# Weight halves ahead of the inner norms, and orders elsewhere, in a two-layer decoder trunk

## The reference

```
for i in range(2):
    y = conv_deltanet_mixer(x, ...) if i == 0 else nsa_mixer(x, positions, ...)
    x = layer_norm(alpha * x + y, ln_mix_g[i], ln_mix_b[i])
    x = layer_norm(alpha * x + (silu(x @ gate) * (x @ up)) @ w_out, ln_ffn_g[i], ln_ffn_b[i])   # 5632 hidden
```

## Time and profile before

| | |
|---|---|
| three runs | 2394.88, 2398.44, 2401.35 us; median 2398.44 |
| profiled execution | 2397.81 us |
| its span, first to last instruction | 2396.0 us |
| PE busy | 2350.1 us (98%) |
| DVE, ACT, POOL busy | 1560.1, 1124.0, 34.9 us |
| TensorE's granted clock, mean | 0.996 |
| read from memory, written | 436.74 MB, 2.11 MB |

### The profile page before, as it was taken

One profiled execution on the slowest core, in us unless ns is written; L12 is line 12 of the kernel. 1 busy time (PEld: TensorE's weight loads), 2 busy tenths in 40 slices (PEclk: granted clock), 3 DMA queues, 4 the chain that ended last, 5 costly groups with the idle time before them and its releaser, 6 DMA issues.

```text
span 2396.0 us, 31921 instructions
## 1 busy us (share of the span) xinstructions
PE 2350.1 (98%) x12225; PEld 2010.3 (84%) x12225; DVE 1560.1 (65%) x2097; ACT 1124.0 (47%) x1516; POOL 34.9 (1%) x79
## 2 busy tenths in 40 slices
PE   8999999999999999999999999999999999999998
PEld 8999988778888888888889888887888888888886
DVE  6767785676666666755587657766766666666556
ACT  4446654454444444444465445546444444444443
POOL 1000000100000000000000000000000000000000
PEclk9999999999999999999999999999999999999999
DMA  7555442735555555655546643245555555565553
GB/s 266 183 186 190 163 141 88 286 138 193 193 193 193 193 193 193 228 193 193 193 161 225 214 161 106 88 158 177 176 199 194 193 191 195 194 218 203 193 193 111
DMA packets 180441, 440.08 MB, mean 184 GB/s; under 512 B 7304, under 2 KB 19728, under 8 KB 166016
## 3 DMA queue, kind: packets, MB, share of 16 engines
q1 hardware_dynamic: 177984, 425.75, 51.2%
q0 software_dynamic: 2368, 13.13, 1.4%
HBM read 436.74 MB, written 2.11 MB: 183 GB/s over the span
## 4 chain that ended last, share of the span: by engine, by line
PE 89%; DVE 6%; ACT 3%; issue 1%; DMA 1%; SPq 0%; DVEq 0%; ACTq 0%
PE bank L1909 28%; PE bank L1911 28%; PE bank L1910 28%; PE bank L2199 1%; DVE w_lo L1177 1%; PE bank L2423 1%; ACT w_hi L669 1%; PE bank L2396 1%; PE bank L2174 1%; DVE stats L1255 1%; DVE x L1254 1%; DVE spare_lo L1177 0%; PE bank L2414 0%; ACT yt L744 0%; DVE yt L1278 0%
## 5 line engine op out<-in xcount | busy, mean ns | idle before, releaser
L1177 DVE TENSOR_TENSOR w_lo<-raw,w_hi 128x1024 fp32r<-128x1024 f32 x774 | 941.5, 1224 | 715.1 <-ACT w_hi L669 712.0
L669 ACT ACTIVATE w_hi<-raw 128x1024 fp32r<-128x1024 f32 x774 | 817.1, 1059 | 1050.2 <-PE bank L1911 1036.9
L1909 PE MATMUL bank<-w_hi,xt_hi 128*128 128x512 f32 x1904 | 746.7, 392 | 3.2 <-DVE xt_lo L1286 1.2
L1911 PE MATMUL bank<-w_hi,xt_lo 128*128 128x512 f32 x1904 | 741.9, 390 | 0.0
L1910 PE MATMUL bank<-w_lo,xt_hi 128*128 128x512 f32 x1904 | 741.8, 390 | 0.0
L1909 PEld LDWEIGHTS bank<-w_hi,xt_hi 128*128 128x128 f32 x1904 | 358.0, 188 | 78.5 <-issue 3.3
L1911 PEld LDWEIGHTS bank<-w_hi,xt_lo 128*128 128x128 f32 x1904 | 357.9, 188 | 75.0
L1910 PEld LDWEIGHTS bank<-w_lo,xt_hi 128*128 128x128 f32 x1904 | 357.9, 188 | 72.5
L1909 PE MATMUL bank<-xt_hi,w_hi 128*128 128x256 f32 x912 | 262.7, 288 | 8.7 <-DVE w_lo L1177 8.7
L1909 PE MATMUL bank<-w_hi,a_hi 128*128 128x512 f32 x672 | 261.4, 389 | 0.0
L1910 PE MATMUL bank<-w_lo,a_hi 128*128 128x512 f32 x672 | 261.4, 389 | 0.0
(11 more groups left out here) (288 smaller groups left out, 1456.6 us busy)
## 6 DMA issues: line engine op xcount, KB each, us to landing
raw<-in_ffn_w_in_dram SPq DMA_DIRECT2D x176, 1024.0 KB, 4.8
raw<-in_ffn_w_out_dram SPq DMA_DIRECT2D x88, 1024.0 KB, 4.9
raw<-in_hy_w_in_dram SPq DMA_DIRECT2D x53, 1024.0 KB, 5.0
raw<-in_nsa_w_in_dram SPq DMA_DIRECT2D x41, 1024.0 KB, 5.1
raw<-in_hy_w_out_dram SPq DMA_DIRECT2D x16, 1024.0 KB, 5.2
raw<-in_nsa_w_out_dram SPq DMA_DIRECT2D x16, 1024.0 KB, 5.1
raw<-in_hy_w_in_dram SPq DMA_DIRECT2D x8, 512.0 KB, 8.0
raw<-in_cmp_w_k_dram SPq DMA_DIRECT2D x4, 1024.0 KB, 5.4
```

The source lines that it names most:

```text
L669: act.activation(weights_of(h)[0], half_of(h), ACT.Copy).then_inc(w_hi_ready, 1)
L1177: dv.tensor_tensor(lo, src, hi.bitcast(F32), ALU.subtract).then_inc(w_lo_ready, 1)
L1909: pe.matmul(dst, l_hi, r_hi, start=start, stop=False, skip_group_check=shared)
L1911: return pe.matmul(dst, l_lo, r_hi, start=False, stop=stop, skip_group_check=shared)
```

## The change

Eight edits, all on the order of work, on where parts lie, or on how a piece of work is cut:

1. Spare slots are 13 single slots of 8 KB for each partition, instead of two blocks of four: they lie in `big`, `a_hi`/`a_lo`, `yt`, and `xt_hi`/`xt_lo`. The table `SPARES` says for each norm which halves lie in which. The first spared half is one earlier (or two, at the second norm) than before. `all_split` is the wait that keeps a spare slot from being written before the activations there are dead.
2. At each inner norm, ACT and DVE split five halves instead of two ahead of the statistics, and fewer behind.
3. Start: SP issues the first half-slab of weights ahead of the first piece of x; ACT and DVE split it ahead of their first piece of x.
4. Delta rule: the transposes to token rows go behind the products by head; the multiply of the keys by the decay goes behind the base solve.
5. `out0`: its first half at column part 1 waits for one tile's two banks at a time, tile 1's first.
6. Value blocks: the sums stand behind nine splits where one stood ahead of them, in two parts with halves between.
7. Attention, first group: `probs_T(0, 0)` goes ahead of `exps(0, 1)` on ACT.
8. End: DVE takes 768 columns of the first tile and GpSimd 1280, without a wait of GpSimd for DVE; DVE subtracts the mean of the second tile's first piece while ACT takes the root.

The core of the diff (left out: helpers that only rename, the imports of offsets, the same moves on the engine that mirrors one shown):

```diff
-        spare_at = (big_at, big_at + 4 * 4096)
-        spare_hi = [sb(f"spare_hi{n}", [P, 4, 1024], F32R, offset=spare_at[n]) for n in range(2)]
-        spare_lo = [sb(f"spare_lo{n}", [P, 4, 1024], F32R, offset=spare_at[n] + 4 * 4096) for n in range(2)]
+        SLOT = 4 * 2048
+        spare_at = [big_at + SLOT * k for k in range(6)] + [a_at] + [at_ + SLOT * k for at_ in (yt_at, xt_at, xt_at + 2 * SLOT) for k in range(2)]
+        spare_hi = [sb(f"spare_hi{k}", [P, 1024], F32R, offset=v) for k, v in enumerate(spare_at)]
+        spare_lo = [sb(f"spare_lo{k}", [P, 1024], F32R, offset=v + SLOT // 2) for k, v in enumerate(spare_at)]
...
-        uses([("ktok", hh) for hh in range(2)] + [("vtok", t, hh) for t in range(NT) for hh in range(2)])
         for t, hh in units:
             uses([("kk", t, hh), ("kq", t, hh)])
+        uses([("ktok", hh) for hh in range(2)] + [("vtok", t, hh) for t in range(NT) for hh in range(2)])
...
+        IN_YT, IN_XT, USUAL = (7, 8), (9, 10, 11, 12), (None,) * HL_SLOTS
+        SPARES = ((*IN_YT, 0, 1, 2, 3, 4, 6, *USUAL, 0, 1), (*IN_XT, 0, 1, 2, 3, 4, *USUAL, 0),
+                  (2, 3, 4, 5, 6, 0, 1, *USUAL, 2, 3, 4), (0, 1, 2, 3))
+        spared, before_in_slot, last_in = {}, {}, {}
+        for (name, kts), slots in zip(OUTER, SPARES):
+            for p, k in enumerate(slots):
+                if k is not None:
+                    h = 2 * (S[name] + kts) - 2 * TAIL + p
+                    spared[h], before_in_slot[h] = k, h - p + slots.index(k) if k in slots[:p] else None
...
-                sp.dma_start(yt[:, v, :], x_by_feature[:, v, :]).then_inc(xt_in[p], 16)
+                if p:
+                    sp.dma_start(yt[:, v, :], x_by_feature[:, v, :]).then_inc(xt_in[p], 16)
                 sp.dma_start(as_in(raw[:, quad, :])[:, 2 * hf:2 * hf + 2, :], cols(w, quad, slice(3 * SC, 3 * SC + CH))[:, 2 * hf:2 * hf + 2, :])\
                   .then_inc((slab_in if hf else first_in)[quad], 16)
+                if p == 0:
+                    sp.dma_start(yt[:, v, :], x_by_feature[:, v, :]).then_inc(xt_in[p], 16)
...
-            pieces = [(0, slice(0, D // 2), out_ready, 1), (0, slice(D // 2, D), out_by_pool, 1)]
+            pieces = [(0, slice(0, FIRST), out_ready, 1), (0, slice(FIRST, D), out_by_pool, 1)]
...
-                cols = slice(D // 2, D)
+                cols = slice(FIRST, D)
                 v = x[:, 0, cols]
                 pool.wait_ge(x_normed, 3 * 4 + 1)
-                pool.wait_ge(out_ready, 1)
...
-                    if slot_before(h) is not None:
-                        act.wait_ge(half_used, at(slot_before(h) + 1, i, per))
+                    if before_in_slot[h] is not None:
+                        act.wait_ge(half_used, at(before_in_slot[h] + 1, i, per))
+                    if h in all_split:
+                        act.wait_ge(a_lo_ready, all_split[h])
...
-            halves(1)
-            for hh in range(2):
-                put(("ktok", hh), k_tok[:, 4 * hh:4 * hh + 4, :])
-            for t in range(NT):
-                for hh in range(2):
-                    put(("vtok", t, hh), v_tok[:, t, 4 * hh:4 * hh + 4, :])
...
-            halves(1)
+            halves(2)
...
+            for hh in range(2):
+                put(("ktok", hh), k_tok[:, 4 * hh:4 * hh + 4, :])
+            halves(1)
+            for t in range(NT):
+                for hh in range(2):
+                    put(("vtok", t, hh), v_tok[:, t, 4 * hh:4 * hh + 4, :])
+            halves(4)
...
             for g in range(NG):
-                exps(g, 1)
-                halves(1)
                 if g:
+                    exps(g, 1)
+                    halves(1)
                     heads_out(g - 1, 1)
-                probs_T(g, 0)
+                    probs_T(g, 0)
+                else:
+                    probs_T(g, 0)
+                    exps(g, 1)
+                    halves(1)
...
             def ln(n):
 
-                halves(2)
+                halves(5)
                 first_moments(n)
                 scale(n, 0)
                 moments(n, 1, 0)
-                halves(1)
                 dv.wait_ge(gb_in, 48 * (n + 1))
                 turned_y(n, 0, 0)
                 moments(n, 1, 1)
                 turned_lo(n, 0, 0)
                 turned_lo(n, 0, 1)
                 moments(n, 1, 2)
-                halves(1)
                 moments(n, 1, 3)
                 turned_lo(n, 0, 2)
                 scale(n, 1)
...
                 turned_lo(n, 0, 3)
                 halves(1)
                 turned_y(n, 1, 0)
-                halves(2)
+                halves(1)
                 turned_lo(n, 1, 0)
                 turned_lo(n, 1, 1)
...
-                result(0, slice(0, D // 2))
+                result(0, slice(0, FIRST))
                 for c in range(4):
                     moments(n, 1, c)
+                dv.wait_ge(var_ready, NT * n + 2)
+                pieces = [x[:, 1, c * CH:(c + 1) * CH] for c in range(4)]
+
+                def centred(c):
+                    own(dv.scalar_tensor_tensor(pieces[c], pieces[c], mv[:, 1, 0:1], gb[:, 0, c * CH:(c + 1) * CH], ALU.subtract, ALU.mult))
+
+                centred(0)
                 inverse(n, 1)
                 for c in range(4):
-                    result(1, slice(c * CH, (c + 1) * CH))
+                    dv.scalar_tensor_tensor(pieces[c], pieces[c], rstd[:, 1:2], gb[:, 1, c * CH:(c + 1) * CH], ALU.mult, ALU.add)\
+                      .then_inc(out_ready, 1)
+                    if c < 3:
+                        centred(c + 1)
...
+            for hh in range(2):
+                wait_sp_read(dv, ("ktok", hh))
+            own(dv.tensor_tensor(k_tok, k_tok, over(kdec, DH), ALU.mult))
...
+            halves(9)
+            chunk_staged(C["vc"])
+            for hf in range(2):
+                block_sum(1, hf)
+                halves(2 - hf)
+            block_hi(1)
             halves(1)
-            block_sum(1)
-            halves(8)
-            block_hi(1)
-            halves(2)
             block_lo(1)
-            halves(6)
+            halves(4)
+            dv.wait_ge(for_pe, FP[("blocks", 1)])
...
+            keys_by_token()
+            z_halves(1)
+            for t in range(NT):
+                values_by_token(t)
+                z_halves(1)
+            z_halves(3)
...
+                    on_small = name == "out0" and col == 1 and kt == 0
+                    for t, cc in ((1, 0), (1, 1), (0, 0), (0, 1)) if on_small else ((0, 0), (1, 0), (0, 1), (1, 1)):
+                        if on_small and cc == 0:
+                            for hh in range(2):
+                                wait_sp_read(pe, ("y", 1 - t, hh))
```

More of the change, by code:

```diff
@@ L1518, in _ @@
             own(dv.scalar_tensor_tensor(nbe, egc, -1.0, beta, ALU.mult, ALU.mult))
-            for hh in range(2):
-                wait_sp_read(dv, ("ktok", hh))
-            own(dv.tensor_tensor(k_tok, k_tok, over(kdec, DH), ALU.mult))
             halves(1)
-            for t in range(NT):
-                for hh in range(2):
-                    wait_sp_read(dv, ("vtok", t, hh))
             n_from = [7]
@@ L2289, in _ @@
             turned_out(1)
-            for hh in range(2):
-                for t in range(NT):
-                    wait_sp_read(pe, ("y", t, hh))
+            assert [K[("y", t, hh)] % 4 for t in range(NT) for hh in range(2)] == [2, 3, 0, 1]
             out_halves(EARLY["out0"])
```

72 lines of the change are left out of this document (34 added, 38 removed).

## The result

The changed kernel took 2379.47 us (median of 6 runs, 2378.64 to 2381.16), against 2398.58 for the kernel before (6 runs, 2394.88 to 2401.35). The ratio is 0.9924, with an interval of 0.9914 to 0.9934: faster by 0.8%, or 19.1 us. Its profiled execution took 2381.16, span 2379.4, so between the two profiled executions the difference is 16.6 us.

What follows compares the result with a forecast made beforehand. TensorE (PE) bounds the kernel, busy 98% of the span, so only its idle 45.9 us and lowered clock can go. Terms 0.1+0.3+9.3+4.3-0.9+0.8 = 13.9 us off 2397.8 gave 2384; 8-in-10 range 2377.5 to 2392.

Steps and rivals of the forecast that it cites:

- the likeliest case: Whole kernel: the forecast as summed, 2384 us, with its own range of 2380 to 2388; chance 0.50.
- the norms' term: Three inner norms: with splits ahead of the statistics, PE's spare low part waits go; 3.1 us per norm, +9.3 in all.
- the level finish: Inner norm: DVE's eleven splits end at 477.9, level with PE's first sum at 477.94.
- Rival B: Inner norms: slabs land too late or two waits stay; 1.0 us per norm instead of 3.1, total 2390; chance 0.14.
- Value blocks: Value row sums moved and cut: 2.96 us stall and 2.85 of low clock go, 1.5 of new waits come; net +4.3.
- Delta rule: Transposes and key multiply moved later: loss of 0.7 us, bounds +1.0 and -2.7; with output halves +0.3 together.
- Rival D: Delta rule and attention: new stalls halve the clock, 1.4 to 2.8 us each on top, total 2388.5; chance 0.14.
- PE's wait ... could end at 316.05: Delta rule, second tile's products: DVE frees the banks 1.26 us earlier, so PE's wait ends at 316.05 instead of 317.31.
- Attention: First attention group: the 0.88 us wait for copies goes, a 1.8 stall comes at scaled heads' transposes; -0.9, bounds +0.9 and -3.5.
- the slack of 1 us: First attention group: PE can absorb 1 us of the 2.8 us delay in DVE's branch scaling, so it stands 1.8.
- Tail: End of the kernel: fewer DVE columns give 0.5 us, the earlier centring 0.3; +0.8, bounds 0.4 and 1.2.
- the rule that I weighed: End: a two-SBUF-input DVE instruction and a GpSimd SBUF read exclude each other; up to 0.4 us lost, saving 13.5 rather than 13.9.

## Why the prediction was right in its range, and what was off

The time, 2379.5, lies in the range of 2377.5 to 2392 and below the likeliest case's own 2380 to 2388: the gain was 19.1 where I had summed 13.9. Of the 5.2 between them, 2.5 are the norms' term, which was too small, and 2.5 the difference between the medians and the profiled executions (below); the other misses nearly cancel.

- **Norms: right in mechanism, mis-sized.** The burst, the level finish (478.11 against 477.9 worked out), the slack at the second tile and the one wait left of 0.3 all came as written. The term "per norm 3.1" measured 3.94, since I took a stall's price to be its recorded idle time. Each costs about 0.26 us more here. The rows show where it lies: matmuls last 0.39 us but start every 0.23, so the last one before a stall still counts as busy for 0.16 after the next would have begun, and the first one behind a stall takes 0.31 instead of 0.23 until the next starts. These two make 0.24; the 0.26 was measured by taking the stalls away and putting them back. Rival B's late slabs came, but as waits of ACT of 0.67 to 0.82, which the burst could bear.
- **Value blocks: right**, 4.24 for 4.3, and in both terms. The same 72 matmuls (from 1296.86 to 1312.49 before, from 1289.13 to 1300.44 after) took 15.6 us and then 11.3. At full clock and without waits they would take about 9.8 us: 56 of them at the 0.94 us for eight that the rows show there, and the last sixteen in 3.2, as before. So the old order lost 5.9 there, for which I had 5.8 (2.96 of stall and 2.85 of low clock), and the new one loses 1.5, for which I had 1.5. Only half of the 1.5 is recorded as idle (0.75); the rest is in that wait's restart and in late starts like the one at 1297.62.
- **Output product's first half: right**, 1.24 for 1.0: the wait of 0.99 is gone in every kernel with the edit, and the other 0.25 has the size of a restart. No run takes this edit out alone.
- **Delta rule: the stall came as worked out, its size moves.** I wrote "a loss of 0.7" with the clock falling as its lower bound. Against the profile of the kernel before it was 2.0 in the profiled execution, 1.8 to 2.4 in the other three with a fall of the clock, and 0.0 to 0.3 in the two of six in which the stall stayed under 2. The average over the old and new orders' profiles is a loss of 1.1; the medians show no loss. Rival D came true here in four of six; in attention, where it gave the stall of 1.8 the same effect, no fall followed the 1.42 in any of the eight profiles that have it. The step "PE's wait ... could end at 316.05" took the transfer's landing for granted, and the landing moves by 1 us.
- **Attention: wrong.** The new stall came where I had put it, at the transposes of the scaled heads, but it was 1.42 and not 1.8, and the wait behind it shrank, which I had not looked at. Before, that one was this row:

```profile
1451.50 0.66 PE L2174 MATMUL bank<-ident,sc_more 128*128 128x128 f32 x4 [0.67 <-ACT big L1085]
```

  With the earlier trace rows the old order stood 0.88+0.67 = 1.55 and the new one 1.42+0.35 = 1.77, and the stretches differ by 0.14. The steps that failed are the slack of 1 us "by my reckoning", by which the stall was 0.4 too long, and the wait behind it, left at its old size.
- **Tail: right**, 0.79 for 0.8, and in its parts: 0.26 for the centring (0.3) and 0.53 for the columns (0.5). At 768 columns the rule that I weighed shows no price: GpSimd's add ends at 2371.12, beside only the first 0.2 us of the centring, which takes its usual 0.75. At 512 the end comes 1.07 later than at 768, more than the whole edit gives.
- **Start:** the first matmul came 0.19 sooner, where I took 0.1, and waits for the low part of x behind the split, as written. At the mark near 285 the two profiles differ by 0.74, but the mark itself scatters more than that, and no run could tell it from nothing.

The sum of the profiled executions, 16.6, is 2.5 below the difference of the medians. The kernel before was profiled 0.8 below its median and the changed one 1.7 above its own. The changed kernel's has two falls of the clock that come in some executions only: in the delta rule (some 1.6) and behind the 1.23 and 0.68 us waits of the fourth attention group, where the stretch to the next wait took 10.9 us in eight of the twelve profiled executions (PEclk 0.72 over six microseconds, as in the earlier trace rows) and 9.3 in four, of which this is one:

```profile
1530.00:1536.00 6.00, 6.00 (x29) 4.98 (x30) 5.97 (x11) 4.13 (x9) 0.00 (x0) 1.00 0.22 41
```

(this row is of the kernel with the delta rule put back, behind the same two waits). The kernel before has the second fall in its profile too, so only the first can account for a part of the 2.5. How often each fall comes in runs without a profile isn't recorded, but every run's mean clock is. The kernel before, in the rounds of the experiments, took 2395.6 to 2396.0 in the five runs with 0.998, 2395.0 to 2400.0 in the six with 0.997, and 2398.0 to 2400.9 in the nineteen with 0.996; the changed one took 2381.2 in its run with 0.997 and 2378.6 to 2379.7 in the five with 0.998 or 0.999. So the scatter goes largely with the clock; which falls make it stays open.

## What to carry to other kernels

Count a stall of a pipelined engine as its recorded idle time plus a restart (0.26 us here), and compare starts of instructions where waits may be shorter than that: many small stalls cost more than they look. Where splits of weights are pure preparation they belong ahead of a section bound by latency, into whatever memory is dead there. Cut a long operation in pieces only after asking whether its place is wrong: here the place was worth nine tenths. Before giving an idle GpSimd more columns, look at which of VectorE's instructions with two SBUF operands will meet it.

## What the runs showed of the hardware

- A stall of 1.6 or 1.9 us left the clock at 1.00, stalls of 2.0 to 3.1 were followed by a lower one (0.50 and 0.52 over the windows behind stalls of 2.96 and 3.07), for some 3 to 7 us. The stall of 1.42 in attention was followed by none, and the same pair of waits (1.23 and 0.68 us) was followed by either, from one execution to the next.
- Each stall of PE at the norms cost 0.26 us beyond its recorded idle time, and in the value blocks late starts and a restart cost 0.8 us beyond the recorded 0.75.
- A centring of DVE with both operands in SBUF stood behind a GpSimd add: 2.02 us instead of 0.75.
- A 1 MB broadcast through memory, issued beside weight slabs, landed 7.4 to 8.2 us after its issue, and the stall of PE behind it went from 1.6 to 2.5 us with the landing, with the low clock behind it in the four executions with 2.0 or more and not in the two with less.
